# Four small edits to a one-core hybrid decoder step: cache slots in plain rotation, keys turned behind the scan's first chunk, output products moved ahead, one more place for expert weights

## What is computed

```
for each sample b:   s = q_lat . lat[pages(b)] + q_rope . krope[pages(b)];  p = softmax(s);  o_lat = p . lat
for each chunk i:    v = u_i - w_i S;  o_i = q_i S + a_i v;  S = S * decay_i + k_i^T v
for each expert e:   y += gate[:, e] * ((lin + 1) * (glu * sigmoid(1.702 glu))) @ w2[e]
```

## Time and profile before

| | us |
|---|---|
| median of 3 runs | 1478.03 (1472.29 to 1478.19) |
| the profiled execution, its own time | 1474.19 |
| its span, first to last instruction | 1472.4 |
| PE, DVE, ACT, POOL busy | 1342.5, 473.3, 175.9, 48.1 |
| mean granted TensorE clock | 0.977 |

### The profile page before, as it was taken

The page is one execution under the profiler, slowest core; times in us unless marked ns, Lnnn a source line. Parts: engine busy times, 40 slices in busy tenths (PEclk is TensorE's granted clock), DMA queues, the critical chain, the costliest instruction groups (busy, mean ns, idle before and its releaser), DMA issues.

```text
span 1472.4 us, 19981 instructions
## 1 busy us (share of the span) xinstructions
PE 1342.5 (91%) x8119; PEld 626.1 (43%) x8119; DVE 473.3 (32%) x1082; ACT 175.9 (12%) x343; POOL 48.1 (3%) x45
## 2 busy tenths in 40 slices
PE   8999887999998989999998998998989989889896
PEld 6667543354586453333333233333332333333322
DVE  1856665932033352132222122122221221222213
ACT  1053101221022430000000000000000000000002
POOL 0000211000000420000000000000000000000000
PEclk9999988999999989999999999999999999999999
DMA  9111553636457669999999999999999999999996
GB/s 372 40 36 76 202 209 150 241 112 256 177 223 232 245 254 426 427 426 428 428 428 428 427 428 428 428 428 428 428 428 427 428 428 427 427 427 427 428 427 249
DMA packets 80339, 490.62 MB, mean 333 GB/s; under 512 B 9308, under 2 KB 14528, under 8 KB 28987
## 3 DMA queue, kind: packets, MB, share of 16 engines
q1 hardware_dynamic: 77690, 468.86, 77.2%
q0 software_dynamic: 2304, 20.97, 3.6%
q10 hardware_dynamic: 296, 0.11, 0.0%
HBM read 483.97 MB, written 6.04 MB: 333 GB/s over the span
## 4 chain that ended last, share of the span: by engine, by line
DMA 43%; PE 21%; DVE 2%; ACT 1%; SPq 1%; POOL 1%; issue 1%; DVEq 0%
DMA arena<-in_w_e 42%; PE ps L2032 12%; PE ps L2075 4%; DMA arena<-in_cache_mem_k 1%; PE ps L2103 1%; SPq L1449 1%; PE ps L2117 1%; PE ps L2087 0%; PE ps L2111 0%; POOL arena L2426 0%; POOL arena L2424 0%; DVE arena L2612 0%; DVE arena L2615 0%; DVE arena L2609 0%; PE ps L2062 0%
## 5 line engine op out<-in xcount | busy, mean ns | idle before, releaser
L2032 PE MATMUL ps<-arena 128*64 128x512 f32 x2048 | 460.6, 597 | 54.0 <-DMA arena<-in_w_e 53.0
L2032 PEld LDWEIGHTS ps<-arena 128*64 128x64 f32 x2048 | 146.3, 137 | 346.7 <-issue 293.9
L2075 PE MATMUL ps<-arena 128*64 128x512 f32 x952 | 209.3, 594 | 0.4 <-ACT arena L2289 0.2
L2075 PEld LDWEIGHTS ps<-arena 128*64 128x64 f32 x952 | 67.6, 137 | 136.3 <-issue 128.4
L2609 DVE TENSOR_SCALAR arena<-ps 128x1024 f32<-128x1024 f32 x15 | 18.4, 1225 | 264.7 <-PE ps L2032 264.7
L2627 DVE TENSOR_TENSOR res<-res,ps 128x512 f32<-128x512 f32 x60 | 41.3, 688 | 135.5 <-PE ps L2087 135.5
L2621 DVE COPY arena<-ps 128x512 f32<-128x512 f32 x15 | 10.4, 692 | 209.6 <-PE ps L2075 209.6
L1073 PE MATMUL ps<-arena 32*4 32x512 f32 x640 | 48.9, 657 | 17.5 <-DVE arena L1099 17.5
L1746 PE MATMUL ps<-arena 128*128 128x512 f32 x128 | 55.8, 594 | 0.0
L2018 PE MATMUL ps<-arena 128*128 128x128 bf16 x768 | 54.0, 223 | 1.7 <-DVE arena L2576 1.7
L2087 PE MATMUL ps<-arena 128*128 128x512 f32 x120 | 55.5, 606 | 0.0
(11 more groups left out here) (554 smaller groups left out, 1357.0 us busy)
## 6 DMA issues: line engine op xcount, KB each, us to landing
arena<-in_w_e SPq DMA_DIRECT2D x383, 1024.0 KB, 22.2
arena<-in_w_in SPq DMA_DIRECT2D x8, 1380.0 KB, 17.6
arena<-in_cache_mem_k SPq DMA_DIRECT2D x8, 1024.0 KB, 9.1
arena<-in_w_out SPq DMA_DIRECT2D x2, 2048.0 KB, 8.2
arena<-in_w_xk SPq DMA_DIRECT2D x1, 4096.0 KB, 15.5
arena<-in_w_xv SPq DMA_DIRECT2D x1, 4096.0 KB, 13.6
arena<-in_w_xq SPq DMA_DIRECT2D x1, 4096.0 KB, 23.1
arena<-in_cache_mem_v SPq DMA_DIRECT2D x1, 4096.0 KB, 16.0
```

What stands on the lines that cost most here:

```text
L2032: last = pe.matmul(ps[64 * x:64 * x + 64, c, :], xe[:, k, 64 * x:64 * x + 64], weights[x][:, c * 512:(c + 1) * 512], start=False, stop=(k ...
L2075: last = pe.matmul(ps[64 * x:64 * x + 64, 6 + c, :], aT[:, k, 64 * x:64 * x + 64], weights[x][:, j * D + c * 512:j * D + (c + 1) * 512], s ...
```

## The change

Four edits. (1) `SLOT` becomes a plain rotation, so sequence 6 goes to slot 2 behind sequence 2 and sequence 7 to slot 3 behind sequence 3, fetched in the order 4, 5, 6, 7; since slot 3 is now in use until the last sequence, group A's half of `w_out` waits for `pv_done` = 8. (2) The last inversion step no longer turns the keys of step 6; chunk 0 of the scan runs first, on DVE and on PE, and then the keys of step 6 are turned and step 6 is done. (3) On PE the group B products of parts 2 and 3 (the second tile of the prompt) move ahead of the wait for group A's half of `w_out`. (4) A fourth one-time place takes fill 20 of the first pair, so the ring's second round in the first pair is 12 to 19; the first three one-time places are filled at the earlier of the two moments.

```diff
-    SLOT = (0, 1, 2, 3, 0, 1, 3, 2)
+    SLOT = (0, 1, 2, 3, 0, 1, 2, 3)
...
-    def pages_dve(dve, k):
+    def pages_dve(dve, k, turn_next=True):
...
-        turn_keys_of(dve, k + 1)
+        if turn_next:
+            turn_keys_of(dve, k + 1)
...
-        pages_dve(dve, level_step(LEVELS))
+        pages_dve(dve, level_step(LEVELS), False)
...
-        for b in (4, 5, 7, 6):
+        for b in range(NSLOT, DEC):
...
-            for k in chunk_steps(i, 0):
+            for k in chunk_steps(i, 0) if i > 0 else ():
                 pages_dve(dve, k)
...
             last.then_inc(s_ready, 1)
+            if i == 0:
+                turn_keys_of(dve, STEP_SCAN)
+                for k in chunk_steps(i, 0):
+                    pages_dve(dve, k)
...
-            for k in chunk_steps(i, 0):
+            for k in chunk_steps(i, 0) if i > 0 else ():
                 pages_pe(pe, k)
...
             last.then_inc(add_made, 1)
+            for k in chunk_steps(i, 0) if i == 0 else ():
+                pages_pe(pe, k)
...
-            sp.wait_ge(sa["pv_done"], DEC - 1)
+            sp.wait_ge(sa["pv_done"], DEC)
             load_w_out(sp, 0)
...
             join_products(pe, 0)
-            pe.wait_ge(gn["placed"], 1)
+            mix_part(2, range(H, 2 * H))
+            pe.wait_ge(gn["placed"], 2)
+            mix_part(3, range(H, 2 * H))
             pe.wait_ge(wout_gdn_loaded, 16)
             mix_part(0, range(H))
...
-            mix_part(2, (*range(H, 2 * H), *range(H)))
+            mix_part(2, range(H))
             join_products(pe, 3)
             turn(pe, 1)
-            mix_part(3, (*range(H, 2 * H), *range(H)))
+            mix_part(3, range(H))
...
-    SPARE = 3
+    SPARE = 4
...
-    spare = (xnT[:, :, :].rearrange("p k n -> p (k n)")[:, 0:2048], arena[:, AT_YE:AT_YE + 2048], arena[:, AT_WOUT + 2048:AT_WOUT + 4096])
+    spare = (arena[:, ARENA - 2048:ARENA], xnT[:, :, :].rearrange("p k n -> p (k n)")[:, 0:2048], arena[:, AT_YE:AT_YE + 2048], arena[:, AT_WOUT + 2048:AT_WOUT + 4096])
...
-            for i in range(2):
+            for i in range(3):
                 fill(sp, FIRST_SPARE + i, 0, spare[i], spare_full[i])
             sp.wait_ge(mo["logits"], 3)
-            fill(sp, FIRST_SPARE + 2, 0, spare[2], spare_full[2])
+            fill(sp, FIRST_SPARE + 3, 0, spare[3], spare_full[3])
```

More of the change, by code:

```diff
@@ L1879, in build @@
     assert AT_YE + 2048 <= AT_WXO + KD * D
-    SPARE = 3
+    SPARE = 4
     FIRST_SPARE = FILLS - SPARE
-    spare = (xnT[:, :, :].rearrange("p k n -> p (k n)")[:, 0:2048], arena[:, AT_YE:AT_YE + 2048], arena[:, AT_WOUT + 2048:AT_WOUT + 4096])
+    assert AT_WXO + KD * D + D // 2 <= ARENA - 2048
+    spare = (arena[:, ARENA - 2048:ARENA], xnT[:, :, :].rearrange("p k n -> p (k n)")[:, 0:2048], arena[:, AT_YE:AT_YE + 2048], arena[:, AT_WOUT + 2048:AT_WOUT + 4096])
     spare_full = [sem(f"spare{i}_full") for i in range(SPARE)]
```

## The result

Over 20 runs each the changed kernel takes 1469.18 us (median, 1462.35 to 1474.63) and the kernel before 1476.4 (1471.72 to 1481.39): ratio 0.995, 95% interval 0.9936 to 0.9964. So 7.2 us are gained between the medians, 5.3 to 9.4 by the interval. The profiled execution takes 1465.33, span 1463.5, 8.9 less than before's; it is one of the quicker ones of its kernel.

The account below looks back on a forecast made before the run. The experts' DMA stream, starting when PE frees its first ring place, was taken as the bound. 9.80 + 0.85 + 0 + 0.9 = 11.55 us gave 1462.6 profiled, 1466.5 on the median; forecast the middle, 1464.6, range 1459 to 1471.

Parts of the forecast that it names:

- What bounds the kernel: Whole kernel: the experts' DMA stream at about 427.5 GB/s plus a fixed tail; time saved ahead moves the whole stream.
- four signs of being wrong: DVE wait over 2 us for sequence 4 or 7, half clock behind chunk 0, PE wait for `w_out`, first expert issue after 540.
- Edit 1: DVE's wait for sequence 6: rotation removes it, saving 7.70 us of wait and 2.10 of half clock, 9.80 in all.
- Sequence 7 pays nothing: Sequence 7's later fetch: lands at 248.0, needed at 250.7, margin 2.7 us, so no cost.
- I take 0.85 since the gap is shorter than either stretch that the old trace slowed in: Chunk 0 first: 0.85 us gained, PE's new 3.3 us idle gap being shorter than the 5 and 7.7 us ones.
- PE cools in the new gap: Rival, behind chunk 0: the 3.3 us idle costs a half-clock stretch, 1.5 to 3.9 us over forecast, about 1467; chance 0.14.
- sequence 4, forecast with 1.9 to spare: POOL's fetch behind step 6's products: sequence 4 lands at 212.7, needed at 214.6, margin 1.9 us.
- Edits 1 and 3, `w_out`: Output projection: moved products cover group A's later load with margin 0.3 us, cost 0; 7.0 without that cover.
- on PE the order changes and the work does not: Output projection: products moved ahead on PE make parts 2 and 3 that much shorter later.
- Edit 4: Start of the expert stream: the fourth place gains 0.9 us, not a full fill's 2.45; ends 0 and 2.45.
- the count of one late release: Expert ring, first to second pair: DMA wants fill 24 at 607.8 and waits until 609.1; dip about 1.3 us.
- The sum: All terms: 9.80 + 0.85 + 0 + 0.9 = 11.55 us; faster by over 0.5% given 0.80.

Follow-up runs that it names:

- e3: The changed kernel with three one-time places instead of four: 1470.15 us, ratio to before 0.9963.
- e11: The changed kernel itself, run and profiled once more with nothing altered: 1467.07 us, ratio to before 0.9954.
- e4: The changed kernel without the moved group B products, so the later `w_out` load is uncovered: 1475.99 us, ratio to before 0.9999.
- e2: The kernel before with only the order changed to chunk 0 ahead of step 6's keys: ratio to before 0.9995.
- e6: The changed kernel, with PE doing three instead of two steps of the next pair's hidden product before combining the last output: 1471.84 us, ratio to before 0.9953.
- e1: The changed kernel with the keys of step 6 turned ahead of chunk 0 again: 1469.47 us, ratio to before 0.9952.
- e12: The changed kernel plus idle products in PE's waits around chunk 0, before sequence 6's small product and the last two sequences' latent products: 1463.2 us, ratio to before 0.9922.
- e7: The changed kernel with the old chunk 0 order, but DVE's new state ahead of the turning that waits for sequence 3: 1469.6 us, ratio to before 0.9928.
- e10: The order of e7 with ten idle products in PE's wait for sequence 3, and three one-time places: 1467.55 us, ratio to before 0.9937.

## Why the prediction was right, and where it was not

**What bounds the kernel**: right. Stream and tail are as long as before, and what the front saves, the end moves. Of the four signs of being wrong that the prediction named, one came: half clock behind chunk 0. DVE's wait for sequence 4 is 1.00 and not over 2, PE has no wait for `w_out`, and the first expert issue is at 537.98.

**Edit 1**: right to 0.1. Between the new states of chunks 1 and 3 it is 38.35 - 28.47 = 9.88 less; the forecast was 9.80, with 7.70 of wait and 2.10 of clock. Sequence 7 pays nothing, as forecast. The other value, 30.11, gives 8.24 in executions whose scores behind the wait of 1.89 run wholly or in part at half clock (5 of the 12 with rotation, 2.61 to 3.56 for 1.93). The kernel before was profiled once, so its own spread in this stretch is not known.

**Edit 2**: the step that failed is "I take 0.85 since the gap is shorter than either stretch that the old trace slowed in". It was the rival "PE cools in the new gap", which had a chance of 0.14, and whose range at the negative maximum, 0.6 gained to 3.0 lost, holds the 1.94 lost here. (Its price in time, "1.5 to 3.9", begins too high: 0.6 gained where 0.85 was forecast is 0.25.) The 3.25 wait slowed the scores in all six executions with edit 2 and no idle products, as the rival had it. What cost the time is a wait that neither forecast nor rival counted: 1.78 ahead of chunk 0's products. Behind it these run at half clock in the profile after, e3 and e11 (1.96 at 193.69), in half in e4, hardly in e2 and not at all in e6. Where they are slow, DVE's state comes late (197.69 + 0.89 and not 196.7), and sequence 4, forecast with 1.9 to spare, is 1.00 late. The negative maximum lies at 16.87 and 16.88 in e2 and e6, at 18.29 to 19.80 in the other four; without edit 2 it lies at 17.78, 17.86, 18.31 and 18.42. On the median that is nothing, e1 and e2 say. In the three executions with edit 2 and PE kept busy it is 17.04 to 17.28, 0.6 to 0.8 less than before: the size that was forecast, under a condition that the change by itself meets in some executions and not in others.

The Trainium skill (TensorE: Matmul & The Clock Gate, Part 1) says of a kernel's start that how many matmuls run cold, and how long they take, differs from run to run of one kernel. The two rows at 225, far behind the start, agree, with 1.93 and 3.56 behind the same wait.

**Edits 1 and 3, `w_out`**: the cover is worth what was forecast (7.04 without it, 0 to 0.4 with it; 0.18 in e12). The step "on PE the order changes and the work does not" holds for the work and not for its clock. The part behind the products of L1368 takes 4.61 to 5.59 in ten executions with the moved products, and 3.60 in the eleventh, e12. In e2 and e4, which keep the old order here, two parts take 7.03, full clock, and in the kernel before 8.11. Why the new order should slow that part, no run shows. PE's longer wait ahead of the last sequence's products, 2.57 for 0.87, and the 3.36 behind it are not the edits' doing: e2, in the old order, waits as long, and e11, in the new one, waits 0.87. In e2:

```profile
308.46 1.93 PE L1087 MATMUL ps<-arena,res 128*32 128x256 f32 x32 [2.56 <-DVE res L1110]
```

It goes with the clock of the part ahead of it, 5.40 in the kernel before and e11, 3.70 in the profile after and e2. The whole stretch grows by 0.8 to 2.1 in most executions with the moved products and by 7.8 to 8.4 in e7, e10 and e11; with the clock at 1.00 throughout, in e12, it shrinks by 1.45.

**Edit 4**: 0.9 forecast, nothing measured. The dip is where it was forecast, 60 us behind the start; the step that failed is the count of one late release, 1.3 us of waiting. The second dip, at 605, was not seen; the two take 1.7, and the 30 us around them 2.2, of the fill's 2.45.

**The sum.** Forecast 11.55; measured 7.2, just short of the 0.5%, 7.4 us, that the prediction called the least that can be told from no change; it gave 0.80 to more than that. The interval is clear of no change all the same. Of the gap 0.85 and 0.9 are edits 2 and 4. The remaining 2.6 is a little over the usual growth of the output's stretch, and the rarer large one is among the runs too; that this adds up to 2.6 on the median is an estimate and not shown. With PE kept at full clock behind the scan (e12) 12 us come out, of which 9.88 is the rotation; some 1.5 of them are half clock that the kernel before had itself in the stretch behind state 3 (83.36 against 81.91).

## What to carry to other kernels

A wait removed pays its length plus the half clock behind it, and both can be read from the rows of the trace before; a wait made or lengthened on TensorE is to be costed with its half clock even if it is under 2 us. Where such a wait cannot be removed, idle products into a free piece of PSUM are cheap to try: e12, with 24 of them, has the lowest median here, while edits 2 and 4 brought nothing that could be measured. And a profile of a kernel with short waits is one draw: before a difference of 2 us in one stage is explained, the same kernel's second profile is the measure of it.

## What the runs showed of the hardware

- The stretches at half clock differ from execution to execution of one program. Of the changed kernel's 20 runs the fastest, 1462.35, has a mean granted clock of 0.985, and those at 1474.3 to 1474.6 have 0.973 to 0.975: about 1 us per 0.001.
- Once low, the clock may stay low while PE works without a pause: 0.50 from 280 to 292 in e11, with PE busy for all of the last 8 us, where another execution of the same program was back at 1.00 by 280.
- Idle products in earlier waits went with full clock at a later place too: in e12's one profile the part at 315.31, behind 3.63 us of products of 4 columns, is at full clock, where it took 4.61 in the profile after, 4.78 in e1 and 5.59 in e11. That the idle products did it is not shown: e2 and e4, in the old order, have full clock there without any.
